# Two attentions of a long transformer kernel: in each round the product with the values is issued ahead of the next turn instead of behind it

## What is computed

```
# first attention: 8 heads, keys of 96 numbers, values of 64, masked by chunks of 64
sc = einsum('bqhd,bkhd->bhqk', q, k) * scale
pr = softmax(where(k_chunk <= q_chunk, sc, neg))
ob = einsum('bhqk,bkhd->bqhd', pr, v)
...
# second attention: 12 heads, keys and values of 64, three results that are gated and added
o = g0 * o_c + g1 * o_s + g2 * o_w        # compressed, selected, window; s and w are causal softmaxes
# and 4 heads that look at a memory of 256 rows, without a mask
o = einsum('bhsm,bmhd->bshd', softmax(einsum('bshd,bmhd->bhsm', q, k)), v)
```

## Time and profile before

| what | us |
|---|---|
| median of the runs | 2093.65 |
| the profiled execution, its own time | 2092.47 |
| its span in the trace | 2090.7 |
| PE busy | 2060.4 (99%) |
| DVE busy | 987.6 (47%) |
| ACT busy | 578.3 (28%) |
| POOL busy | 1281.9 (61%) |
| first attention, from its first scores to the next stage's first matmul | 252.5 to 292.75 |
| second attention, the same | 1546.1 to 1671.2 |

### The profile page before, as it was taken

The page is one execution under the profiler, slowest core; times in us unless marked ns, Lnnn a source line. Parts: engine busy times, 40 slices in busy tenths (PEclk is TensorE's granted clock), DMA queues, the critical chain, the costliest instruction groups (busy, mean ns, idle before and its releaser), DMA issues.

```text
span 2090.7 us, 30074 instructions
## 1 busy us (share of the span) xinstructions
PE 2060.4 (99%) x10222; PEld 1671.6 (80%) x10222; DVE 987.6 (47%) x1729; ACT 578.3 (28%) x1144; POOL 1281.9 (61%) x850
## 2 busy tenths in 40 slices
PE   8999999999999999999999999999999999999997
PEld 6888768888888887899788888888975588888886
DVE  4452464655552055466455555234367635555311
ACT  3211343422220054322342222000237632222100
POOL 6666637866667668432656666676555565666663
PEclk9999999999999999999999999999999999999999
DMA  5322373333333343221133323334410033332332
GB/s 178 100 90 91 95 96 118 111 93 98 100 101 110 101 143 95 77 62 41 51 93 98 99 91 101 101 111 131 141 51 2 11 91 93 98 100 91 101 111 70
DMA packets 55316, 195.24 MB, mean 93 GB/s; under 512 B 5923, under 2 KB 6115, under 8 KB 54980
## 3 DMA queue, kind: packets, MB, share of 16 engines
q1 hardware_dynamic: 49968, 179.85, 27.9%
q10 hardware_dynamic: 5268, 14.30, 3.2%
HBM read 188.10 MB, written 6.03 MB: 93 GB/s over the span
## 4 chain that ended last, share of the span: by engine, by line
PE 58%; issue 1%; DVE 1%; ACT 0%; POOL 0%; POOLq 0%; DVEq 0%; ACTq 0%
PE acc L832 16%; PE acc L835 16%; PE acc L836 16%; PE acc L1124 2%; PE sc L1143 2%; PE pp L1161 2%; PE acc L1358 1%; PE acc L902 0%; PE pp L1168 0%; DVE s_m L2025 0%; PE acc L1075 0%; PE acc L977 0%; PE acc L1280 0%; PE pp L1030 0%; PE sc L1336 0%
## 5 line engine op out<-in xcount | busy, mean ns | idle before, releaser
L715 POOL TENSOR_TENSOR wlo<-wraw,whi 128x1024 fp32r<-128x1024 f32 x334 | 805.9, 2413 | 27.9
L713 POOL TENSOR_SCALAR whi<-wraw 128x1024 fp32r<-128x1024 f32 x334 | 354.2, 1060 | 646.9 <-PE acc L832 596.5
L832 PE MATMUL acc<-xhi,whi 128*128 128x512 f32 x1776 | 697.3, 393 | 11.8 <-POOL wlo L726 9.6
L835 PE MATMUL acc<-xhi,wlo 128*128 128x512 f32 x1776 | 692.2, 390 | 0.0
L836 PE MATMUL acc<-xlo,whi 128*128 128x512 f32 x1776 | 692.1, 390 | 0.0
L832 PEld LDWEIGHTS acc<-xhi,whi 128*128 128x128 f32 x1776 | 334.0, 188 | 88.3 <-issue 13.8
L836 PEld LDWEIGHTS acc<-xlo,whi 128*128 128x128 f32 x1776 | 333.9, 188 | 70.3
L835 PEld LDWEIGHTS acc<-xhi,wlo 128*128 128x128 f32 x1776 | 334.0, 188 | 67.8 <-issue 0.2
L832 PE MATMUL acc<-fhi,whi 128*128 128x512 f32 x528 | 205.4, 389 | 0.0
L835 PE MATMUL acc<-fhi,wlo 128*128 128x512 f32 x528 | 205.4, 389 | 0.0
L836 PE MATMUL acc<-flo,whi 128*128 128x512 f32 x528 | 205.4, 389 | 0.0
(11 more groups left out here) (383 smaller groups left out, 2431.9 us busy)
## 6 DMA issues: line engine op xcount, KB each, us to landing
wraw<-in_weights SPq DMA_DIRECT2D x335, 512.0 KB, 3.6
distances<-vr ACTq DMA_DIRECT2D x1, 3840.0 KB
toep<-distances ACTq DMA_DIRECT2D x4, 768.0 KB, 9.6
h<-in_x_t SPq DMA_DIRECT2D x4, 512.0 KB, 7.9
mem<-in_mem_t ACTq DMA_DIRECT2D x2, 1024.0 KB, 15.0
w<-in_weights ACTq DMA_DIRECT2D x1, 2048.0 KB, 11.1
out_t<-h SPq DMA_DIRECT2D x8, 256.0 KB, 2.2
dmf<-in_sums ACTq DMA_DIRECT2D x1, 576.0 KB, 6.0
```

The costliest lines, as they stand in the source:

```text
L713: nc.gpsimd.tensor_scalar(whi[:, j, :], wraw[:, j % RAW, :], 1.0, 1.0, ALU.mult, ALU.mult).then_inc(sem["w_hi"], 1)
L715: nc.gpsimd.tensor_tensor(wlo[:, j, :], wraw[:, j % RAW, :], plain(whi[:, j, :]), ALU.subtract).then_inc(sem["w_split"], 1)
L832: m = nc.tensor.matmul(o, a_hi, b_hi, start=start, stop=False)
L835: nc.tensor.matmul(o, a_lo, b_hi, start=False, stop=False)
```

## The change

In the loop of `attention` two lines change places. At step g PE now issues the product of step g - 8 first, then the turn of step g - 7, then the scores. Nothing else differs: all instructions, waits, banks and buffers are the same, and the lists of DVE, ACT, POOL and SP are the same row for row.

```diff
             for g in plan.steps():
+                values(g - V_LAG)
                 turn(g - T_LAG)
-                values(g - V_LAG)
                 scores(g)
```

## The result

The changed kernel takes 2109.22 us in the median of 4 runs (2108.61 to 2109.64), the kernel before 2093.76 us (2092.67 to 2094.14). That is 15.5 us more; the ratio is 1.0074, 95% interval 1.0063 to 1.0086. In microseconds the interval is 13 to 18 more. The forecast was 2108.3 us, 14.7 us more, with a range of 2102 to 2114.

A forecast was written before the change was run, and what follows sets the result against it. PE was taken as the bound, inside the attentions too, each wait paid in full. Steady rounds 7.5 + drains 3.3 and 3.9 = 14.7 us on the median 2093.65 gave 2108.3 us, range 2102 to 2114.

The forecast's parts named there:

- The time from a turn to its product, 1.94 us: Both attentions: a product may start 1.94 us behind its turn's start (1.13 to DVE's copy, 0.69 copy, 0.12 to PE).
- the two bounds: Price of a product's wait: 11.3 us in all if the 0.12 costs nothing, 18.3 if the first weight load lies open.
- Product 1, 12 x 0.50: Steady rounds: turn 1 and short scores cover 1.44 of 1.94 us, so 0.50 of waiting at 12 places, 6.0 us.
- Products next to memory scores, four times 0.29: Steady rounds: products 0 and 1 behind 256-key memory scores wait about 0.29 us at four places, 1.2 us.
- Product 2, 0.03: Steady rounds: turn 2 and scores over 256 keys cover 1.22 of 1.25 us; 0.03 ten times, 0.3 us.
- The drains, 3.3 and 3.9: Ends of the attentions, without scores as cover: 3.3 us more in the second, 3.9 in the first.
- POOL's chain: Next couple's turn 0 waits for POOL behind DVE's later copy; expected not to bind by 0.3 us; rival 2112, chance 0.08.
- Product 0 is covered: Steady rounds: turn 0 and scores over 512 keys cover 2.09 us, more than 1.94, so no wait, 0.15 to spare.
- a copy that finds DVE still at its scores: Such a copy starts later than 1.13 us behind its turn; may add some tenths in couples that carry a result.
- Nothing behind takes it back: Stages behind the attentions recover none of the loss, since PE is the bound there as well.
- The clock: Slower clock booked at 0; as rival, it falls in the drains, 29 us more in all, 2122, chance 0.03.
- the copies are there in time: Rival: copies ready within 1.44 us of turn 1's start, no steady wait, 2093.1 us; chance 0.09.

## Why the prediction was right

The mechanism held: products wait for their copies at the forecast places, PE pays each wait in full, and nothing later takes it back. Its terms one by one:

- *The time from a turn to its product, 1.94 us.* Measured 1.96 to 1.97 to the matmul's start, in the 12 steady couples: the 0.12 from copy to PE holds for these products as it did for a turn, and 0.03 of the first weight load lies open. Of the two bounds the measured price lies next to the middle that was taken.
- *Product 1, 12 x 0.50.* 0.53 us each in the second attention. In the first a couple takes 0.40 us more from turn 0 to turn 0 (10.11 against 9.71), as its scores are longer; the forecast had called 0.50 the most there.
- *Products next to memory scores, four times 0.29.* Waits of 0.3 us, as forecast.
- *Product 2, 0.03.* It was 0.06, and 0.6 us over ten couples instead of 0.3.
- *The drains, 3.3 and 3.9.* Measured 3.5 and 4.1, by putting the old order back.
- *POOL's chain.* It was to have 0.3 us to spare. In causal couples it did not bind. At one turn, the one behind the two memory couples, it did, for 0.17 us (1597.10 to 1598.30 is 1.20 instead of 1.03).
- *Product 0 is covered.* This step failed at two places, 0.18 and 0.44 us, by late scores as above. It is the term that was too small, together with the 0.03: the forecast named it ("a copy that finds DVE still at its scores") and gave it no value. The trace before holds it already: at the first of the two places turn 1 stood behind the long scores, at 1583.81, 1.14 us behind their start at 1582.67 instead of 1.06, since DVE came to its copy only at 1583.33, 1.68 behind its turn:

```profile
1581.65 1.09 PE L1143 MATMUL sc<-const,s 128*128 128x128 f32 x8
...
1583.33 0.69 DVE L1724 COPY pt<-sc 128x512 f32<-128x512 f32 x1
```
- *Nothing behind takes it back.* It held: the lengths of the dense stages differ by the clock as told above and don't shrink by what the attentions lose.
- *The clock.* For the waits that the change makes it held. The matmuls in the drains have the lengths of the steady rounds and the granted clock is 1.00. The row on which the term was built is weaker than it looked: the same wait of 2.34 us is followed by the lower clock in the changed kernel and in five others. What carries the term is that waits of 0.9 us at most, five of them in 16 us, brought no fall in any trace; a fall in both drains would have cost some 14 us by the price of that rival. The Trainium skill says in "TensorE: Matmul & The Clock Gate", Part 1, that a TensorE which idles often between groups of matmuls swings between its two clocks. The traces don't agree with it for the drains; behind the wait of 2.34 us six of ten show a fall.

Of the rivals, "the copies are there in time" falls with the 27 waits, the clock with the drains, and POOL's chain was worth 0.2 us. In sum 14.7 us were forecast and 15.5 measured; an interval of 13 to 18 can't tell these two apart, so part of the closeness is chance. The traces are sharper: their 16.25 us hold 0.8 of the late copies and POOL, 0.3 at product 2 and about 0.4 in the drains more than the forecast, and the rest is rounding.

## What to carry to other kernels

In an order written out by hand, measure the time from a producer's start to the moment when its consumer may go on (here 1.94 us: the turn, a copy, the handing over), and count what the bounding engine has to do between the two in each place of the round; the shortest place decides, and it can be a place that the moved operation is not part of. An instruction that is moved ahead of another changes the cover of both, and of whoever waits for the bank. If an order has to change, change the distance with it: the same order with the products one step further back cost nothing.

## What the runs showed of the hardware

- Two float32 matmuls on 64 columns of the array each run side by side: 1.01 us together, and 1.00 for the second alone when the first had started 0.5 us sooner.
- From the end of a copy on DVE to the weight load on PE that waits for it, 0.115 us passed where an instruction that only waits stood ahead of the load, and 0.05 where the load itself waited for it.
- PE's matmuls kept the upper clock through a drain of 15.8 us with five waits of 0.6 to 0.9 us, nearly all of the rest transposes and half-width products. At one wait of 2.34 us, the same in all ten traces, the clock fell to the lower level in six of them: matmuls over 512 columns took 0.63 us instead of 0.40 there.
